# Seven-product blocks whose pairs are added in PSUM: a decoder layer in split float32 on one core

## Chip, cores and metric

One core of one Trainium2 chip runs the whole kernel. The metric is the device time of one execution in microseconds (us), lower is better; the median of three runs of the kernel before is 1603.2 us (1603.16 to 1603.54).

## What is computed

One decoder layer on 1024 prompt tokens and 8 single-token samples (width 1024, hidden width 2816), all in float32:

```python
z = xn @ w_in                       # 1024 x 7168; xn = rms_norm(x)
u, v, b_gate, c_gate, x_in, r_a, r_b = split(z)
y_a = (gelu(u) * spatial_mix(layer_norm(gelu(v)))) @ w_a_out
y_b = (b_gate * short_conv(c_gate * x_in)) @ w_b_out
h = sigmoid(r_a) * y_a + sigmoid(r_b) * y_b
x = x + rms_norm(h @ w_o)
f = (silu(xf @ w_gate) * (xf @ w_up)) @ w_down      # xf = rms_norm(x)
x = x + rms_norm(f)
```

The outputs are the layer's result for prompt and samples, the last rows of the convolution input, and the normed v of the samples.

## The kernel before

**Arithmetic.** Each float32 operand is split in two parts of reduced width, hi and lo. A product takes three passes on TensorE (hi x hi, hi x lo, lo x hi). ScalarE writes hi of the weights and of late operands (`hi`, line 1240, and `t_split`, line 1583), GpSimd writes lo of the weights (`rest`, line 1095), VectorE writes lo of the operands (`t_rest`, line 2385, and others of that form).

**Blocks.** A large product is cut in blocks of 256 weight columns. Each block is a two by two product of half matrices. A seven-product block does it with seven products instead of eight (Strassen's scheme in Winograd's form); it needs sums of the weight quarters (`sums`, lines 1822 to 1841, VectorE) and sums of the operand's quarters, called totals. A plain block does eight (`half`, four results of two products each). The plain blocks are the first two u blocks, B_A, B_B, B_F and B_UP0, and the first block of each of the three down sets, B_D, B_D+4 and B_D+8. A run is one pass over a block; the last down block is done in two runs of half size. A product on 2 x 258 columns with kp = 4 takes 4 x 3 x 2 = 24 matmuls, one with kp = 3 takes 18, one of a half-size run 12.

**Results of a seven-product run.** The seven products 0 to 6 go to the four PSUM regions in the order PBANK = Z, W, Y, X, Z, Y, X. ScalarE copies product 0 to SBUF (`s1`, line 1251). VectorE then adds, each time with one operand from PSUM: `c11` (line 1847), `u1` (1853), `u3` (1858), `u2` (1864), `c22` (1869), `c12` (1875), `c21` (1880). TensorE waits in `product`: product 4 for `s1`, product 5 for `c11`, product 6 for `u1`; the first use of a region by a new block waits for what read it last (`bank_free`).

**Order.** Every engine has its program written out by hand, with semaphores. What matters here:

- ScalarE, run after run: `s1(r)`, then hi of the seven weight places of the next block (`prepare`), the last of which waits for product 6 of run r; between these come what the stage wants of it (gelu, sigmoid, silu, splits, in the last down set `sq_gain`). In the last r_b run (B_A-1) `a_split(1)` stands ahead of `s1`; in block B_B `bt_split(3)` and a weight part stand ahead of `s1(B_B+1)`; at the third block of a down set `t_split` of the next set's first operand stands ahead of `s1`; in the last down set the last `sq_gain` of a block, which waits for its `c21`, stands ahead of the next `s1`, and before the last run a table load too.
- VectorE: in the last r_b run `a_rest(0)`, `at_total(0)`, `c11`, `a_rest(1)`, `u1`, `u3`, `at_total(1)`, `u2`, `a_rest(2)`, `c22`, `c12`, `c21`. In the up runs it multiplies with silu (`hidden`, line 2420) and forms the totals of the hidden rows (`hidden_total`, line 2394) after `c21`.
- The down product is summed over three sets of hidden rows, kp = 3, 4, 4 (K_FIRST). The operands of a set, four rows and four totals, come back from DRAM into eight slots of SBUF, 516 KB in each of two transfers, while the set before ends (`operand_load`, line 976, on SyncE's queue), are split by ScalarE (`t_split`) and VectorE (`t_rest`). In sets 1 and 2 the block's results are added to the sums in g (`gather`, line 2484).
- In the last half-size run TensorE sums the squares of the first half's result after product 3 (`y_total`, line 735); `y_root_of` on VectorE (2526 to 2530) follows, ahead of `u2` of that run.

## Time and profile before

| | |
|---|---|
| median of three runs | 1603.2 us |
| profiled execution | span 1601.0 us, and 2.2 us around it to the median |
| PE busy | 1590.6 us, 99% |
| DVE busy | 1081.9 us, 68% |
| ACT busy | 559.8 us, 35% |
| POOL busy | 703.9 us, 44% |
| chain that ended last | PE 95%, of it line 414 (the three-pass matmuls) 91% |
| granted TensorE clock | 0.999 of full speed over the span |

PE is TensorE, DVE VectorE, ACT ScalarE, POOL GpSimd; SP's queue issues the transfers. Line 414 is the matmul of `three`. The chain is followed back from the last instruction, so an engine that stands in it at 95% has next to no wait in front of it.

### The profile page before, as it was taken

The numbers are of one execution on the slowest core, as the hardware profiler recorded it, in microseconds if no ns is written. First come the engines' busy times: TensorE is split into PE (matmuls) and PEld (weight loads), VectorE is DVE, ScalarE is ACT, GpSimd is POOL, SyncE is SP. The second block draws the span as 40 slices with busy tenths as digits, with TensorE's granted clock in tenths as the row PEclk, the third lists the DMA queues.
The fourth block names the chain that finished last, engine by engine and source line by source line (L and its number), as shares of the span: only waits on it lengthen the run. The fifth ranks groups of instructions, "written<-read, shape, count | busy, mean of one in ns | idle before, by whom it ended". The sixth has DMA issues, their size and how long they took to land.

```text
span 1601.0 us, 30253 instructions
## 1 busy us (share of the span) xinstructions
PE 1590.6 (99%) x12427; PEld 1542.2 (96%) x12427; DVE 1081.9 (68%) x1463; ACT 559.8 (35%) x852; POOL 703.9 (44%) x512
## 2 busy tenths in 40 slices
PE   9999999999999999999999999999999999999998
PEld 6889999999999999999978999999999999999997
DVE  8757857797793338868965666766666666575766
ACT  4222332222223336333434532333332233352544
POOL 1011534544544444644730324544444443545375
PEclk9999999999999999999999999999999999999999
DMA  6202011431423333474423313533333345472723
GB/s 216 79 1 80 27 54 34 126 96 44 126 82 110 109 106 121 149 242 133 148 91 120 131 41 110 155 105 100 106 104 104 105 124 178 153 239 80 238 107 133
DMA packets 155283, 184.38 MB, mean 115 GB/s; under 512 B 7355, under 2 KB 138035, under 8 KB 155147
## 3 DMA queue, kind: packets, MB, share of 16 engines
q1 hardware_dynamic: 154987, 182.41, 35.7%
q8 instruction: 99, 1.62, 0.4%
q14 instruction: 37, 0.30, 0.1%
q10 hardware_dynamic: 160, 0.04, 0.0%
HBM read 133.74 MB, written 48.72 MB: 114 GB/s over the span
## 4 chain that ended last, share of the span: by engine, by line
PE 95%; DVE 1%; DMA 1%; POOL 1%; issue 1%; SPq 0%; ACT 0%; DVEq 0%; ACTq 0%; POOLq 0%
PE ps L414 91%; PE ps L449 1%; PE ps L526 1%; DMA pre_gain<-in_mix_pre_g 1%; DVE tp L2213 1%; PE ps L669 0%; PE ps L653 0%; PE ps L424 0%; DMA tp_f<-hid_dram 0%; SPq L783 0%; DVE s_bc L2232 0%; POOL ring_lo L1108 0%; POOL ring_lo L1095 0%; PE ps L503 0%; DVE g L2234 0%
## 5 line engine op out<-in xcount | busy, mean ns | idle before, releaser
L414 PE MATMUL ps<-tp,ring_hi 128*128 128x258 f32 x7292 | 1182.9, 283 | 0.5 <-issue 0.3
L414 PEld LDWEIGHTS ps<-tp,ring_hi 128*128 128x128 f32 x7292 | 1010.6, 190 | 0.9 <-issue 0.5
L414 PE MATMUL ps<-tp,ring_lo 128*128 128x258 f32 x3646 | 744.8, 283 | 0.0
L414 PEld LDWEIGHTS ps<-tp,ring_lo 128*128 128x128 f32 x3646 | 571.3, 190 | 0.0
L1095 POOL TENSOR_TENSOR ring_lo<-ring_f,ring_hi 128x512 fp32r<-128x512 f32 (+1 forms) x228 | 328.3, 1460 | 365.1 <-DVE ring_f L1840 212.5
L1095 POOL TENSOR_TENSOR ring_lo<-stage,ring_hi 128x512 fp32r<-128x512 f32 (+1 forms) x199 | 304.7, 1540 | 400.3 <-ACT ring_hi L1240 399.6
L1240 ACT ACTIVATE ring_hi<-ring_f 128x512 fp32r<-128x512 f32 (+1 forms) x228 | 142.6, 627 | 519.9 <-DVE ring_f L1835 196.2
L1240 ACT ACTIVATE ring_hi<-stage 128x512 fp32r<-128x512 f32 (+1 forms) x199 | 122.0, 617 | 121.1 <-PE ps L414 63.5
L1832 DVE TENSOR_TENSOR ring_f<-stage 128x512 f32<-128x512 f32 (+1 forms) x57 | 46.8, 821 | 135.2 <-PE ps L414 82.7
L1853 DVE TENSOR_TENSOR s_a<-ps,s_a 128x516 f32<-128x516 f32 (+1 forms) x58 | 39.8, 686 | 51.9 <-PE ps L414 51.4
L414 PE MATMUL ps<-tp 128*128 128x512 f32 (+1 forms) x384 | 72.0, 340 | 0.0
L414 PEld LDWEIGHTS ps<-tp 128*128 128x128 f32 x384 | 59.0, 189 | 8.2
L2385 DVE TENSOR_TENSOR tp<-tp_f,tp 128x2064 fp32r<-128x2064 f32 (+1 forms) x24 | 56.2, 2343 | 13.7 <-ACT tp L1583 13.7
L1251 ACT ACTIVATE s_a<-ps 128x516 f32<-128x516 f32 (+1 forms) x58 | 34.2, 590 | 77.3 <-PE ps L414 60.2
L1864 DVE TENSOR_TENSOR s_a<-ps,s_a 128x516 f32<-128x516 f32 (+1 forms) x58 | 39.6, 683 | 30.5 <-PE ps L414 30.4
L1583 ACT ACTIVATE tp<-tp_f 128x2064 fp32r<-128x2064 f32 (+1 forms) x24 | 42.8, 1784 | 39.8 <-DMA tp_f<-hid_dram 33.2
L414 PE MATMUL ps<-wv_hi_t,tp 128*128 128x512 f32 x192 | 54.1, 397 | 0.0
L2420 DVE TENSOR_TENSOR hq<-hq,q 128x516 f32<-128x516 f32 x40 | 47.0, 1176 | 1.1
L1835 DVE TENSOR_TENSOR ring_f<-ring_f,stage 128x512 f32<-128x512 f32 (+1 forms) x57 | 42.8, 751 | 2.2 <-PE ps L414 2.2
L414 PEld LDWEIGHTS ps<-wv_hi_t,tp 128*128 128x128 f32 x192 | 35.7, 188 | 8.0
L1837 DVE TENSOR_TENSOR ring_f<-stage 128x512 f32<-128x512 f32 (+1 forms) x57 | 39.6, 695 | 0.0
L1847 DVE TENSOR_TENSOR s_bc<-ps,s_a 128x516 f32<-128x516 f32 (+1 forms) x21 | 14.0, 668 | 36.8 <-PE ps L414 36.6
(243 smaller groups left out, 1453.9 us busy)
## 6 DMA issues: line engine op xcount, KB each, us to landing
stage<-in_w_in SPq DMA_DIRECT2D x24, 1024.0 KB, 5.9
ht_dram<-ht SPq DMA_DIRECT2D x44, 258.0 KB, 4.2
hid_dram<-hq SPq DMA_DIRECT2D x40, 258.0 KB, 3.1
stage<-in_w_gate SPq DMA_DIRECT2D x10, 1024.0 KB, 6.6
stage<-in_w_up SPq DMA_DIRECT2D x10, 1024.0 KB, 5.3
tp_f<-hid_dram SPq DMA_DIRECT2D x16, 516.0 KB, 5.5
tp_f<-ht_dram SPq DMA_DIRECT2D x16, 516.0 KB, 8.7
stage<-in_w_down SPq DMA_DIRECT2D x8, 1024.0 KB, 7.1
```

The lines of the kernel that those rows point to most:

```text
L414: ins = pe.matmul(o, w, xc, start=first and n == 0, stop=last and n == 2)
L1095: pool.tensor_tensor(lo, src, hi.bitcast(f32), SUB).then_inc(w_lo, 1)
L1240: act.activation(w_ring(b, p, kp)[0], src, ACT.Copy).then_inc(w_hi, 1)
L1251: act.activation(s_a[:, gs], reg(Z, gs), ACT.Copy).then_inc(s1_done, 1)
L1583: act.activation(slot(s, 0, both, ks), slot_f(s, 1, both, ks), ACT.Copy).then_inc(t_hi, 1)
L1832: ins = dve.tensor_tensor(out, a21, a22, ADD)
L1835: ins = dve.tensor_tensor(out, ring(ring_f, b, 1, kp), a11, SUB)
L1837: ins = dve.tensor_tensor(out, a11, a21, SUB)
L1853: dve.tensor_tensor(s_a[:, gs], reg(X, gs), s_a[:, gs], ADD).then_inc(u1_done, 1)
L1864: dve.tensor_tensor(s_a[:, gs], reg(Z, gs), s_a[:, gs], ADD).then_inc(u2_done, 1)
L2385: dve.tensor_tensor(slot(s, 1, both, ks), slot_f(s, 1, both, ks), slot_v(s, 0, both, ks), SUB).then_inc(t_lo, 1)
L2420: dve.tensor_tensor(hq[:, n], hq[:, n], q[:, n], MUL).then_inc(hid_ready, 1)
```

## The change

- **Regions.** PBANK becomes Y, W, Y, Z, X, Z, X. Product 2 is added by TensorE onto product 0 in Y, after `s1` has copied product 0; product 6 is added onto product 4 in X, after `c22` has read it. So `c11` is no addition any more: the region is read where its value is used (ScalarE's gelu, sigmoid, silu or copy, or VectorE's multiplication or the addition into g). `u1`, `u3`, `u2` and `c22` become `u2`, `u4` and `c22`: five additions of a run for seven. The copies of `s1` alternate between two buffers (`s_turn`).
- **Waits.** Product 2 waits for `s1`, product 5 for `u2`, product 6 for `c22`.
- **Order of products.** Where a seven-product run follows on another (`piped`), product 0 of the next run stands ahead of product 6 of this one.
- **Down blocks.** B_D, B_D+4 and B_D+8 become seven-product blocks. The operand slots form a wheel: position p of a set goes into the slot that position p-1 of the set before left. The loads, `t_split` and `t_rest` follow the positions. In sets 1 and 2 three additions of SBUF onto SBUF (the parts onto g) stand between `u4` and `c22`, and the last addition of each result goes straight into g.
- **Two additions change place:** `at_total(1)` in the last r_b run behind `c22`, and the last tap of the convolution in a b run behind `c22`.

The diff, cut to its core:

```diff
-PBANK = [Z, W, Y, X, Z, Y, X]
+PBANK = [Y, W, Y, Z, X, Z, X]
+D_WHEEL = [5] + SLOTS_B
+SLOTS_D = [[D_WHEEL[(p - n) % 8] for p in range(7)] for n in range(3)]
-QORDER.update({b: FIRST_HALF_EVEN for b in (B_D, B_D + MP, B_D + 2 * MP)})
+def piped(run):
+    return 2 < run < len(RUNS) - 1 and RUNS[run][0] not in QORDER and RUNS[run + 1][0] not in QORDER
...
             def product(r, p):
+                if p == 6 and piped(r):
+                    issue(r + 1, 0)
+                if p or not piped(r - 1):
+                    issue(r, p)
+
+            def issue(r, p):
                 b, gs = RUNS[r]
                 pe.wait_ge(w_lo, lo_at(b, p))
-                if p == 4:
+                if b in (B_D, B_D + MP, B_D + 2 * MP):
+                    pe.wait_ge(t_lo, 7 * ((b - B_D) // MP) + p + 1)
+                if p == 2:
                     pe.wait_ge(s1_done, SIDX[r])
                 elif p == 5:
-                    pe.wait_ge(c11_done, SIDX[r])
+                    pe.wait_ge(u2_done, SIDX[r])
                 elif p == 6:
-                    pe.wait_ge(u1_done, SIDX[r])
+                    pe.wait_ge(c22_done, SIDX[r])
...
-                                kp == 0, kp == kps(b) - 1)
+                                kp == 0 and p not in (2, 6), kp == kps(b) - 1, p in (2, 6))
...
-                act.activation(s_a[:, gs], reg(Z, gs), ACT.Copy).then_inc(s1_done, 1)
+                act.activation(s_turn[r % 2][:, gs], reg(Y, gs), ACT.Copy).then_inc(s1_done, 1)
...
                 if last:
                     a_rest(1)
-                u1(r)
-                u3(r, q[:, 1])
+                u2(r)
+                u4(r, q[:, 1])
                 sums(r + 1, 1)
                 if last:
+                    a_rest(2)
+                c22(r, q[:, 3], q[:, 1])
+                sums(r + 1, 2)
+                if last:
                     at_total(1)
-                u2(r)
-                if last:
-                    a_rest(2)
-                c22(r, q[:, 3])
-                sums(r + 1, 2)
                 c12(r, q[:, 1])
...
+                dve.tensor_tensor(c_22, c_22, s_c[:, gs], ADD).then_inc(d_part, 1)
+                dve.tensor_tensor(c_12, c_12, s_c[:, gs], ADD).then_inc(d_part, 1)
+                dve.tensor_tensor(c_21, c_21, s_turn[r % 2][:, gs], ADD).then_inc(d_part, 1)
+                dve.wait_ge(prod_done, done(r, 4))
+                dve.wait_ge(d_part, parts + 1)
+                dve.tensor_tensor(c_22, reg(X, gs), c_22, ADD).then_inc(c22_done, 1)
```

New in ScalarE's program: `c11_act` (gelu, sigmoid, silu or copy of region Y). The places of `a_split`, `bt_split(3)`, the last `sq_gain` and the table load ahead of `s1` are as before; `t_split` of the first operand of a set still stands ahead of `s1` of the last block before it. In block B_D `t_rest` of position 5 stands ahead of `u2`, and that of position 6 behind `u4`.

## Rows read from the trace of the kernel before

**Rows 1.** The page's head and PE's share.
```profile
span 1601.0 us, 30253 instructions
...
PE 1590.6 (99%) x12427; PEld 1542.2 (96%) x12427; DVE 1081.9 (68%) x1463; ACT 559.8 (35%) x852; POOL 703.9 (44%) x512
```
**Rows 2.** The chain in order of time: start us, us, what.
```profile
199.54 303.78 PE ps L414 x2520
...
1421.17 157.82 PE ps L414 x1308
```
**Rows 3.** PE's waits: us in total, times, longest us.
```profile
PE ps L414 <- POOL ring_lo L1108: 0.3, 1, 0.3
```
**Rows 4.** ACT in order of time, 608 to 612: start us, us, line, operation.
```profile
608.36 0.64 ACT L1342 ACTIVATE q<-q 128x516 f32<-128x516 f32 x1
608.90 1.99 ACT L1337 ACTIVATE tp<-gv 128x1024 fp32r<-128x1024 f32 x2
...
610.90 0.58 ACT L1251 ACTIVATE s_a<-ps 128x516 f32<-128x516 f32 x1
```
**Rows 5.** DVE in order of time, 607 to 625.
```profile
607.63 0.70 DVE L1880 TENSOR_TENSOR q<-ps,s_a 128x516 f32<-128x516 f32 x1 [1.53 <-PE ps L414]
611.03 2.50 DVE L2088 TENSOR_TENSOR tp<-gv,tp 128x1024 fp32r<-128x1024 f32 x2 [2.70 <-ACT tp L1338]
...
620.81 3.45 DVE L2100 TENSOR_TENSOR tp_f<-gv,tp_f 128x1024 f32<-128x1024 f32 x2
```
**Rows 6.** ACT in order of time, 739 to 742.
```profile
739.23 1.92 ACT L1394 ACTIVATE tp<-tp_f 128x2064 fp32r<-128x2064 f32 x1
...
741.57 0.58 ACT L1251 ACTIVATE s_a<-ps 128x516 f32<-128x516 f32 x1
```
**Rows 7.** DVE in order of time, `u1` of the last b run.
```profile
787.02 0.70 DVE L1853 TENSOR_TENSOR s_a<-ps,s_a 128x516 f32<-128x516 f32 x1 [0.74 <-PE ps L414]
```
**Rows 8.** DVE in order of time, the rest of an operand in the last a run.
```profile
706.20 2.31 DVE L2153 TENSOR_TENSOR tp<-tp_f,tp 128x2064 fp32r<-128x2064 f32 x1 [1.66 <-ACT tp L1390]
```
**Rows 9.** DVE in order of time: `c21` and last totals of two up runs.
```profile
987.40 0.70 DVE L1880 TENSOR_TENSOR hq<-ps,s_a 128x516 f32<-128x516 f32 x1 [0.92 <-PE ps L414]
...
992.76 2.59 DVE L2394 TENSOR_TENSOR ht<-hq,ht 128x516 f32<-128x516 f32 x2
...
1352.28 0.69 DVE L1880 TENSOR_TENSOR hq<-ps,s_a 128x516 f32<-128x516 f32 x1
...
1355.74 1.51 DVE L2394 TENSOR_TENSOR ht<-hq,ht 128x516 f32<-128x516 f32 x2
```
**Rows 10.** The instructions on tile tp_f, 1330 to 1530: duration ns min/median/max.
```profile
L2385 DVE TENSOR_TENSOR tp<-tp_f,tp x24: 1759/2304/3404, 1342.6 to 1523.9; 128x2064 fp32r<-128x2064 f32 x16, 128x1548 fp32r<-128x1548 f32 x8
```
**Rows 11.** ACT in order of time, 1400 to 1402.
```profile
1400.00 1.92 ACT L1583 ACTIVATE tp<-tp_f 128x2064 fp32r<-128x2064 f32 x1
1401.82 0.57 ACT L1251 ACTIVATE s_a<-ps 128x516 f32<-128x516 f32 x1
```
**Rows 12.** DVE in order of time, `c21` of the last full-size and first half-size run.
```profile
1563.27 0.70 DVE L1880 TENSOR_TENSOR s_bc<-ps,s_a 128x516 f32<-128x516 f32 x1 [0.99 <-PE ps L414]
...
1573.30 0.43 DVE L1880 TENSOR_TENSOR s_bc<-ps,s_a 128x258 f32<-128x258 f32 x1 [0.51 <-PE ps L414]
```
**Rows 13.** ACT in order of time, ahead of the last two `s1`.
```profile
1565.82 0.71 ACT L1634 ACTIVATE g<-g,par 128x516 f32<-128x516 f32 x1
1566.43 0.37 ACT L1251 ACTIVATE s_a<-ps 128x258 f32<-128x258 f32 x1
...
1575.43 1.28 ACT L1692 ACT_TABLE_LOAD   x1
...
1576.83 0.37 ACT L1251 ACTIVATE s_a<-ps 128x258 f32<-128x258 f32 x1
```
**Rows 14.** The first sum of squares on PE, and DVE after its root.
```profile
1578.84 0.95 PE L735 MATMUL ps<-ones,q 128*128 128x1 f32 x8
...
1581.46 0.43 DVE L1864 TENSOR_TENSOR s_a<-ps,s_a 128x258 f32<-128x258 f32 x1
```

More of the change, by code:

```diff
@@ L87, in places @@
         return [3, 4, 5, 6]
-    return [0, 1, 2, 3] if b in QORDER else list(range(7)) if B_UP0 < b < B_D else TURNED
+    return [0, 1, 2, 3] if b in QORDER else list(range(7)) if b > B_UP0 else TURNED
 def freed(b, pos):
@@ L409, in _, with three @@
         def _(pe):
-            def three(outs, w_h, w_l, x_h, x_l, first, last):
+            def three(outs, w_h, w_l, x_h, x_l, first, last, onto=False):
                 ins = None
@@ L413, in three @@
                     for o, xc in zip(outs, x):
-                        ins = pe.matmul(o, w, xc, start=first and n == 0, stop=last and n == 2)
+                        ins = pe.matmul(o, w, xc, start=first and n == 0, stop=last and n == 2, skip_group_check=onto)
                 return ins
@@ L2483, in gather, with down_rest @@
-            def gather(m, b, src, gs, ready):
-                dve.tensor_tensor(g[:, m, b, gs], g[:, m, b, gs], src[:, gs], ADD).then_inc(ready, 1)
-            def down_rest(r, ready, count, n=None):
-                b, gs = RUNS[r]
-                m = 2 * ((b - B_D) % MP)
-                nb = b + 1 if r < R_LAST else B_D
+            def down_rest(r, n=None, first=None):
+                b, gs = RUNS[r]
+                run = r - FIRST_RUN[B_D + MP]
+                m, parts = 2 * ((b - B_D) % MP), 3 * run
+                nb = b + 1 if r < R_LAST else None
+                c_11, c_12, c_21, c_22 = (g[:, m + a, c, gs] for a, c in ((0, 0), (0, 1), (1, 0), (1, 1)))
+                if first is not None:
+                    t_rest(first, 4)
@@ L2490, in down_rest @@
                 sums(nb, 0)
                 if n is not None:
[L2492 to L2499 removed]
+                    t_rest(n, 0)
+                dve.wait_ge(prod_done, done(r, 2))
+                dve.tensor_tensor(c_11, reg(Y, gs), c_11, ADD).then_inc(d_c11, 1)
@@ L2500, in down_rest @@
+                if first is not None:
+                    t_rest(first, 5)
+                u2(r)
+                u4(r, s_c[:, gs])
                 sums(nb, 1)
+                if first is not None:
+                    t_rest(first, 6)
                 if n is not None:
-                    t_rest(n, 4)
+                    t_rest(n, 1)
                 if r > R_LAST:
                     y_root_of(0)
-                u2(r)
-                dve.wait_ge(ready, count + 1)
-                c22(r, s_b[:, gs])
+                dve.wait_ge(u4_done, SIDX[r])
@@ L2511, in down_rest @@
-                dve.wait_ge(c22_done, SIDX[r])
-                gather(m + 1, 1, s_b, gs, ready)
-                c12(r, s_c[:, gs])
+                    t_rest(n, 2)
+                dve.wait_ge(prod_done, done(r, 5))
+                dve.wait_ge(d_part, parts + 2)
+                dve.tensor_tensor(c_12, reg(Z, gs), c_12, ADD).then_inc(c12_done, 1)
                 sums(nb, 3)
-                dve.wait_ge(c12_done, SIDX[r])
-                gather(m, 1, s_c, gs, ready)
-                dve.wait_ge(ready, count + 2)
@@ L2518, in down_rest @@
-                c21(r, s_b[:, gs])
-                dve.wait_ge(c21_done, SIDX[r])
-                gather(m + 1, 0, s_b, gs, ready)
+                if n is not None:
+                    t_rest(n, 3)
+                dve.wait_ge(prod_done, done(r, 6))
+                dve.wait_ge(d_part, parts + 3)
+                dve.tensor_tensor(c_21, reg(X, gs), c_21, ADD).then_inc(c21_done, 1)
             def y_root_of(n):
@@ L2558, in _ @@
                 sums(b + 1, 2)
-                if last:
-                    t_rest(1, 6)
+                if mp == MP - 1:
+                    t_rest(1, 2)
                 c12(r, g[:, m, 1])
                 sums(b + 1, 3)
+                if mp == MP - 1:
+                    t_rest(1, 3)
+                if mp == 0:
+                    dve.wait_ge(hid_saved[2], 16 * J)
                 c21(r, g[:, m + 1, 0])
-            t_end(1, FIRST_RUN[B_D + MP])
-            for i in range(3):
-                down_rest(FIRST_RUN[B_D + MP + 1 + i], d_tmp, 4 * i, 2 if i == 2 else None)
```

501 lines of the change are left out of this document (260 added, 241 removed).

## Prediction

> **What bounds the kernel now.** I read the page first: TensorE is busy for 1590.6 of 1601.0 us [rows 1]. A busy row alone says little, so the chain in order of time comes next. It is one unbroken stretch of line 414 after the other: 2520 matmuls in 303.78 us, and 1308 in 157.82 us near the end [rows 2]. That is 0.1205 us a matmul in either, without a gap. TensorE's own waits confirm it: three of 0.3 us at line 414, one of which stands here, are all that the matmuls waited between start and tail [rows 3]. So each matmul taken away is worth 0.1205 us, and nothing done to DVE, ACT or POOL can gain more than these 0.9 us. What the change can lose is any wait that becomes too short. With 0.1205 us, a product of 24 matmuls takes 2.89 us, one of 18 (set 0 of down) 2.17, one of 12 (the two last runs) 1.45.
>
> **What it removes.** The three plain down blocks have eight products and get seven: (3 + 4 + 4) x 6 = 66 matmuls, 66 x 0.1205 = **7.95 us**. Of the three small waits two stand at the change of sets, where the order is new, one in the o stage behind DVE, which sheds two additions a run: I take all three as gone, 0.85 us, together **8.8 us**. The two additions fewer on DVE (0.7 us each [rows 5]) lie beside the matmuls and give nothing by themselves. A product that is added onto another has the same matmuls, so it is costed at nothing.
>
> **What it adds: shorter waits.** Before, product 4 needed `s1`; its copy had four products of time. Now product 2 needs it, and the next run's product 0 stands ahead of this run's product 6. So counted from the end of product 6 (call it E), `s1` has exactly one product: 2.89, 2.17 or 1.45 us. ACT's queue ahead of `s1` decides. In an ordinary run that is the last weight part (it waits for E) and `s1`, some 1.2 us: enough. Products 5 and 6 have one product's time for `u2` and (where the next product 0 comes between) two for `c22`; in an ordinary run DVE is idle there. So the bulk of the kernel should run as before. The places with more in the queue:
>
> - *Last r_b run.* ACT has sigmoid, `a_split(1)`, `s1`, and sigmoid waits for `c21`. Before, `c21` began at 607.63 and `s1` ended at 610.90 + 0.58 = 611.48 [rows 4, 5], 3.9 us after E. All of it hangs on E, which moves with the order; 3.9 - 2.89 = **1.0 us** lost. Then `a_rest(0)`, `at_total(0)`, ACT's `at_split(0)`, sigmoid, `a_split(2)`, DVE's `a_rest(2)` and `c22` follow each other, 9 us on from there plus 2.5 to 3.5 us for `a_rest(2)` (the two lengths that operations of this size have) [rows 5], while product 6 would start 12.5 us after E: 0.5 to 1.5 us, taken **1.4**, as POOL prepares weights just then. Last, `at_total(1)` now stands ahead of `c12`, and the following plain block begins in region Z, which `c12` frees: 2.4 (or 4.6) + 0.7 against one product of 2.89, so 0.2 to 2.4, taken **0.3**.
> - *Last a run.* The rest of an operand ends at 706.20 + 2.31 = 708.5 [rows 8], `c22` behind it at 709.2. From `u1` at 787.0 [rows 7], four products into its run, I count back two runs, the plain block and a product: product 6 wants to start at 708.9. **0.4** (0 to 0.5).
> - *First b run.* It follows a plain block, so its `s1` has product 1 alone. By the same counting back product 1 ends at 740.7; `s1` ended at 741.57 + 0.58 = 742.15, after `bt_split(3)` [rows 6]. **1.5** (1.4 to 1.6).
> - *Up into down.* DVE now has in the last up run five `t_rest` for three, then `sums`, `t_rest(5)`, `u2` in B_D. Counting back from 1421.17 [rows 2] B_D began at 1351.9; position 5 is now due at 1362.9. I lay DVE's operations after each other from product 2 (1340.5) on with 0.6 to 0.7 us for one of 516 columns and 1.76 us for a `t_rest` of 1548 [rows 10]: `u2` ends at 1363.0. The same end of an up run (`c21` to last total) took 4.9 us before the plain block, with POOL nearly idle, and 7.9 us where POOL had seven weight places to prepare [rows 9]. B_D has seven now, with three quarters of the columns, and with a drawn-out first part too `u2` ends at 1366.3. 0.1 to 3.4, taken **1.6**.
> - *`t_split` ahead of `s1`* at the last block of set 0: at 1400.00 it took 1.92, `s1` ended at 1402.39 [rows 11]; E was at 1399.5, so 2.9 us against 2.17: **0.8**. At the last block of set 1 against 2.89: **0.15**.
> - *Sets 0 to 1 and 1 to 2.* ACT's `t_split(4)`, behind weight sums that wait for DVE, ends in `s1` some 0.3 to 1.5 us late the first time, 0 to 0.5 the second; DVE's load is seven `t_rest` of 2.3 to 3.4 us [rows 10], three additions and all else, in two blocks: `c22` of the first block may be up to 1.4 late. Taken **1.1** and **0.2**.
> - *Into the half-size runs.* `c21` began at 1563.27 [rows 12]. Without the gather it is followed at 0.75 by square and gain, then `s1` of 0.37: ready 2.4 us after E (spacing as in rows 13), against 1.45: **0.95**. Into the last run the queue is `c21` (0.43 [rows 12]), square, gain, table load 1.28 [rows 13], `s1`: 3.15 us after E against 1.45: **1.7**.
> - *Root before `c22`.* DVE came out of the root at 1581.46, 2.6 us after the sum began at 1578.84 [rows 14]. Now three additions and `c22`, 4 x 0.44, stand behind it, so product 6 can go at 4.4 us, but TensorE is there at 0.94 + 2 x 1.45 = 3.85: **0.6**.
>
> The sum is 2.7 + 0.4 + 1.5 + 1.6 + 0.95 + 1.3 + 2.65 + 0.6 = **11.7 us**; the low ends give 7.3, the high ends some 19.5.
>
> **Transfers.** A set with kp = 4 brings seven operands of 2 x 516 KB where it brought eight, but they are wanted within one block. The slot of position p comes free seven to eight products before it is wanted, 18 us; the trace landed one in 5.5 us, and six with the weights fill some 22 us of a window of 29, so the queue on SP doesn't end last. If it did, each late operand would show as ACT waiting in `t_split`.
>
> A port shared by DVE and POOL fits the two lengths: a two-input SBUF operation took 1.5 us for two when POOL was idle, 2.6 beside it [rows 9]. The Trainium skill states it as an exclusive lock (SBUF — State Buffer, the section on the shared port pair), under which an operation that reads PSUM isn't held up. This speaks against this change: it takes away additions that read PSUM and moves `t_rest` and gathers, which read SBUF twice, under POOL's seven weight parts. By the rule alone the up-to-down place costs towards 3.4 and the set changes towards their high ends, by the undisturbed rows near nothing; the trace agrees with it in the rows named.
>
> **Sum.** Against the profiled span: 1601.0 - 8.8 + 11.7 = 1603.9. The median stands 2.2 above the span: **1606.2 us**, 3.0 above 1603.2. What this kernel's measurement can tell from no change I take as 0.2%, 3.2 us: 1600.0 to 1606.4. The forecast is in that band, at its upper edge.
>
> **Rivals.**
> 1. *Low ends everywhere* (ACT and DVE meet no POOL at the critical places): 1603.2 - 8.8 + 7.3 = 1601.7. For it: several of my late operations are late by under 0.5 us.
> 2. *The waits hold* and the matmuls taken away are the result: 1603.2 - 8.8 = 1594.4; with only the tail's stalls (3.3 us) 1597.7. For it: TensorE's queue is in front by whole products nearly everywhere. Against it: the ACT rows of three places put `s1` behind its date on rows alone.
> 3. *DVE falls behind at the operand changes* (the other side: slower). One mechanism: seven `t_rest`, drawn from 2.3 to 3.4 us beside POOL, ahead of `u2` and `c22`. In two blocks of 40.5 us DVE has some 37 us of work; with all `t_rest` long it is 45, and from the point where it exceeds 40.5 TensorE waits for it block by block: 3 to 4 us at each of the two set changes and 3.4 at B_D, in place of 2.9 in all, so 1606.2 + 7 = 1613.
> 4. *It doesn't do what it says*: were the down blocks' seventh products late by their operands, the 66 matmuls would be paid back as ACT's waits for DMA, 1611. The 18 us of lead speak against it.
>
> **How the numbers follow.** Forecast (1603.5 to 1609) 0.42; rival 1 (1600 to 1603.5) 0.18; rival 2 (under 1600) 0.20; rivals 3 and 4 (over 1609) 0.15 and 0.05. Of the forecast's chance a little over half lies below 1606.4. So faster 0.20, same 0.40, slower 0.40. The range takes in rival 3 and the upper part of rival 2: 1598 to 1613.
>
> **What the profile after would show.** TensorE: 66 matmuls fewer, and in its waits rows at line 414's successor for ACT's copy (`s1`) in the last r_b run, the first b run and both half-size runs, about 1.0, 1.5, 0.95 and 1.7 us; for DVE's `c22` in the last r_b run and the last run, and for `t_rest` or `u2` in B_D. The bulk, from 230 to 600 us and in the up blocks, shows no wait. The prediction is wrong if TensorE waits in ordinary runs (then each of some 50 runs pays), or if `s1` comes in time at the places named (then 1597 or less).

## The result and the profile after

The changed kernel takes **1625.2 us** (median of four runs, 1624.2 to 1626.9) against 1603.4 us (1603.2 to 1603.6) for the kernel before on the same chip: a ratio of 1.0136, 95% interval 1.0121 to 1.0150. It is slower by 22 us, where I had forecast 1606.2 and a range of 1598 to 1613. The time lies outside the range, 12 us above its upper end. The runs further down were made on several chips, on which the kernel before took 1603.4 to 1604.1 us; each ratio is to the kernel before on its own chip.

The head of the page after, then pieces of its chain (start us, us, what):

```profile
span 1622.5 us, 30039 instructions
PE 1590.2 (98%) x12361; PEld 1539.0 (95%) x12361; DVE 999.9 (62%) x1371; ACT 556.4 (34%) x865; POOL 714.1 (44%) x521
```
```profile
199.32 304.00 PE ps L430 x2520
503.43 107.08 PE ps L430 x888
...
628.59 71.19 PE ps L430 x576
703.36 8.33 DMA tp_f<-ob_dram
716.74 32.08 PE ps L430 x264
...
922.03 428.23 PE ps L430 x3552
```

Against [rows 1], TensorE has the 66 matmuls fewer (12361 for 12427), and VectorE 82 us less work. Its busy time fell by 0.4 us only, where 66 matmuls are 8: part of the matmuls must have run slower. The first long piece is that of [rows 2]: the same 2520 matmuls, 304.00 us for 303.78. The up blocks are one piece too, 3552 matmuls at 0.1206 us. So the pairs added in PSUM and the new order of products cost nothing that can be seen in an ordinary run. What is new comes after 600 us: the chain is cut in pieces, and between them stand a transfer, VectorE and ScalarE. The kernel before had three waits of 0.3 us there (one of them in [rows 3]); now TensorE's waits are (us in total, times, longest us):

```profile
PE ps L430 <- ACT s_bc L1308: 5.5, 6, 1.5
PE ps L430 <- DVE g L2550: 4.7, 3, 2.2
PE ps L430 <- ACT s_a L1308: 4.2, 3, 1.8
PE ps L430 <- DVE s_a L1932: 3.3, 1, 3.3
PE ps L430 <- DVE s_a L1943: 2.5, 1, 2.5
PE ps L430 <- DVE q L1943: 2.3, 1, 2.3
```

L1308 is `s1`, L1932 `u2`, L1943 and L2550 the two forms of `c22`. These are 15 waits, 22.5 us, where the prediction had 11.7. The four that I had most wrong or that matter below, one by one (in brackets the wait and what ended it):

```profile
628.59 0.73 PE L430 MATMUL ps<-tp,ring_hi 128*128 128x258 f32 x4 [2.29 <-DVE q L1943]
716.74 0.72 PE L430 MATMUL ps<-tp,ring_hi 128*128 128x258 f32 x4 [2.51 <-DVE s_a L1943]
1376.00 0.73 PE L430 MATMUL ps<-tp,ring_hi 128*128 128x258 f32 x4 [3.27 <-DVE s_a L1932]
1539.20 0.72 PE L430 MATMUL ps<-tp,ring_hi 128*128 128x258 f32 x4 [2.18 <-DVE g L2550]
```

Stretches of 8 us around them (us, PE busy (instructions), granted clock, DMA share, GB/s):

```profile
616.00:624.00 8.00, 8.00 (x69) 1.00 0.35 108
624.00:632.00 8.00, 5.71 (x40) 0.86 0.33 106
632.00:640.00 8.00, 8.00 (x64) 0.92 0.38 134
712.00:720.00 8.00, 5.49 (x46) 1.00 1.10 352
1376.00:1384.00 8.00, 8.00 (x54) 0.79 0.27 86
1448.00:1456.00 8.00, 5.78 (x37) 0.79 0.04 12
```

This is the second part of the loss. After three of the waits the granted clock falls to the lower of its two levels (1.2 GHz for 2.4) for a while: the window from 1376 us is busy all through and does 54 matmuls instead of 69. (1 - 0.79) x 8 is 1.7 us, and (0.14 + 0.08) x 8 as well. In the kernel before no window between 200 and 1590 us was under 1.00.

The books: 1601.0 (span before) - 7.95 - 0.85 + 22.5 of waits + 5.1 for three falls gives 1619.8; 1622.5 was measured. Of the 2.7 us still missing the restarts after the other twelve waits make 2.6. A restart is what a wait costs besides itself where the clock stays up, 0.22 us by the held copies below; in the price of a fall, 1.7 us, it is contained.

### The profile page after: what moved, and what is told of

Same layout as the page of the kernel before. It is cut to its first block, busy times and chain, and to the rows that moved or that the text cites. A ratio compares the mean times of both kernels' runs of the same rounds, so it can differ in the third digit from the quotient of the medians.

```text
span 1622.5 us, 30039 instructions
## 1 busy us (share of the span) xinstructions
PE 1590.2 (98%) x12361; PEld 1539.0 (95%) x12361; DVE 999.9 (62%) x1371; ACT 556.4 (34%) x865; POOL 714.1 (44%) x521
## 4 chain that ended last, share of the span: by engine, by line
PE 89%; DVE 5%; issue 2%; ACT 2%; DMA 1%; POOL 0%; SPq 0%; DVEq 0%; ACTq 0%; POOLq 0%
PE ps L430 84%; DVE tp L2446 2%; PE ps L465 2%; PE ps L542 1%; DMA tp_f<-ob_dram 1%; PE ps L714 0%; PE ps L698 0%; ACT tp L1658 0%; PE ps L440 0%; DVE g L2545 0%; DMA gv<-in_w_in 0%; DVE ring_f L1920 0%; ACT tp L1410 0%; ACT q L1717 0%; ACT ring_hi L1278 0%
## 5 line engine op out<-in xcount | busy, mean ns | idle before, releaser
L1133 POOL TENSOR_TENSOR ring_lo<-ring_f,ring_hi 128x512 fp32r<-128x512 f32 (+1 forms) x240 | 348.4, 1473 | 354.7 <-DVE ring_f L1925 211.3
L1133 POOL TENSOR_TENSOR ring_lo<-stage,ring_hi 128x512 fp32r<-128x512 f32 (+1 forms) x196 | 293.8, 1509 | 416.1 <-ACT ring_hi L1278 415.7
L1278 ACT ACTIVATE ring_hi<-ring_f 128x512 fp32r<-128x512 f32 (+1 forms) x240 | 150.0, 625 | 536.3 <-DVE ring_f L1920 179.3
L1917 DVE TENSOR_TENSOR ring_f<-stage 128x512 f32<-128x512 f32 (+1 forms) x60 | 58.1, 969 | 102.2 <-DMA stage<-in_w_in 52.0
L1954 DVE TENSOR_TENSOR q<-ps,s_a 128x516 f32<-128x516 f32 x17 | 11.8, 696 | 72.2 <-PE ps L430 72.2
L1922 DVE TENSOR_TENSOR ring_f<-stage 128x512 f32<-128x512 f32 (+1 forms) x60 | 52.3, 871 | 0.0
L1932 DVE TENSOR_TENSOR s_bc<-ps,s_bc 128x516 f32<-128x516 f32 (+1 forms) x31 | 21.3, 686 | 47.0 <-PE ps L430 46.9
L1932 DVE TENSOR_TENSOR s_a<-ps,s_a 128x516 f32<-128x516 f32 (+1 forms) x30 | 20.5, 685 | 42.7 <-PE ps L430 42.7
L1925 DVE TENSOR_TENSOR ring_f<-stage,ring_f 128x512 f32<-128x512 f32 (+1 forms) x60 | 40.3, 671 | 0.0
L1658 ACT ACTIVATE tp<-tp_f 128x2064 fp32r<-128x2064 f32 (+1 forms) x21 | 37.4, 1780 | 6.1 <-DMA tp_f<-hid_dram 4.7
L1949 DVE TENSOR_TENSOR q<-ps,q 128x516 f32<-128x516 f32 x24 | 16.7, 694 | 26.6 <-PE ps L430 26.6
```

Source lines behind the costliest of these rows:

```text
L1133: pool.tensor_tensor(lo, src, hi.bitcast(f32), SUB).then_inc(w_lo, 1)
L1278: act.activation(w_ring(b, p, kp)[0], src, ACT.Copy).then_inc(w_hi, 1)
L1658: act.activation(slot(s, 0, both, ks), slot_f(s, 1, both, ks), ACT.Copy).then_inc(t_hi, 1)
L1917: ins = dve.tensor_tensor(out, a21, a22, ADD)
L1922: ins = dve.tensor_tensor(out, a11, a21, SUB)
L1925: ins = dve.tensor_tensor(out, a12, ring(ring_f, b, 3, kp), SUB)
```

## The theories

**Theory A**: the loss is local. At 15 places a step that now has one product of time stands in a queue behind work that used to have four, and after some waits the clock falls too. **Rival B**: the PSUM pairs or the order of products cost something throughout. **Rival C** (rival 3 of the prediction): VectorE has too much to do at the changes of operands. **Rival D** (close to rival 4): transfers are late. Since all the waits are queue order by theory A, it can be tested by moving work alone: e1 to e5, e8 and e9 issue the same operations as the changed kernel, in another order.

## Three queues, one at a time, and together

ScalarE's order (e1), at the seven places of `s1`; two of them:

```diff
-                if last:
-                    a_split(1)
                 s1(r)
                 if last:
+                    a_split(1)
                     a_split(0)
...
             s1(R_LAST)
-            for e in range(12, 16):
+            for e in range(11, 15):
                 sq_gain(e)
-            act.activation(warm, eps, ACT.Sqrt)
             s1(R_LAST + 1)
+            sq_gain(15)
+            act.activation(warm, eps, ACT.Sqrt)
```

> ScalarE's order alone is changed: at seven places the copy of the first product (s1) is issued ahead of a split, a square or a table load that stood before it; nothing is added or taken out. Theory A (the loss lies in waits at single places, each made by what is queued ahead of one step): the waits of 1.14, 1.47, 0.95, 0.28, 0.22, 1.44 and 1.81 us go, 7.3 us; those of 1.41 and 0.99 us at the two changes of operands go too, but VectorE's queue there is without a gap, so its waits of 2.22 and 2.18 us grow by as much. Time 1617.5 us (1615 to 1620). Rival B (the pairs in PSUM or the new order of products cost time all along the loops): the waits seen are not the loss, 1623 to 1625. No fall of the granted clock was behind these waits, so the windows with 0.79 to 0.92 stay.

Measured: 1622.0 us (1620.5 to 1622.6), ratio to before 1.0112 (1.0097 to 1.0128), so 3 us better than the changed kernel, not 7 to 8. All nine waits of `s1` were gone or under 0.3 us. But TensorE then met the next late step:

```profile
628.87 0.72 PE L430 MATMUL ps<-tp,ring_hi 128*128 128x258 f32 x4 [3.62 <-DVE q L1946]
1452.18 1.20 PE L430 MATMUL ps<-tp,ring_hi 128*128 128x258 f32 x4 [3.14 <-DVE g L2553]
1538.31 1.20 PE L430 MATMUL ps<-tp,ring_hi 128*128 128x258 f32 x4 [3.21 <-DVE g L2553]
```

These were 2.29, 2.22 and 2.18 us: VectorE's chain has its own date, and what TensorE doesn't wait for `s1` it waits for `c22`. The wait for the late load (716.7 us) grew from 2.51 to 2.94 us as well. The sum of waits fell by 5.0 us only, and the longer waits now all had a fall of the clock behind them, five places instead of three. That the changes of sets would hand a wait on I had foreseen, for 628 us not, and the two new falls not at all.

VectorE's order (e2), its main edits:

```diff
-                if last:
-                    a_rest(2)
                 c22(r, q[:, 3], q[:, 1])
+                if last:
+                    a_rest(2)
...
                 dve.tensor_tensor(c_22, c_22, s_c[:, gs], ADD).then_inc(d_part, 1)
-                dve.tensor_tensor(c_12, c_12, s_c[:, gs], ADD).then_inc(d_part, 1)
-                dve.tensor_tensor(c_21, c_21, s_turn[r % 2][:, gs], ADD).then_inc(d_part, 1)
                 dve.wait_ge(prod_done, done(r, 4))
                 dve.wait_ge(d_part, parts + 1)
                 dve.tensor_tensor(c_22, reg(X, gs), c_22, ADD).then_inc(c22_done, 1)
+                if first is not None:
+                    sums(nb, 1)
+                dve.tensor_tensor(c_12, c_12, s_c[:, gs], ADD).then_inc(d_part, 1)
+                dve.tensor_tensor(c_21, c_21, s_turn[r % 2][:, gs], ADD).then_inc(d_part, 1)
```

> VectorE's order alone: in the last r_b run the addition of C_22 ahead of the third operand's rest; three totals of the hidden rows behind the first down block's second addition; in the down blocks the additions for C_12 and C_21 (and, at the two changes of operands, one weight sum) behind that of C_22. Theory A: the waits of 2.29, 3.27, 2.22 and 2.18 us go (9.7 us with 0.3 us of the last run's), and where three of them stood (all but the 2.18) the granted clock no longer falls, some 5 us more: 1610 us (1608 to 1614). If the falls of the clock are not made by the waits: 1615. Rival C (VectorE is short of time at the changes, whatever its order): the waits move to the next product and 1620 to 1625 is left.

Measured: 1622.2 us (1620.8 to 1622.5), ratio 1.0114 (1.0101 to 1.0128): 3 us, where theory A promised 15. The waits named did go (`c22` at 1452 and 1539 us wholly, `u2` from 3.27 to 0.76), and three came: 2.30 us for `c12` at 631.8 us, behind the `a_rest(2)` that I had moved in front of it; 1.56 us for `c22` in the first down block; and

```profile
1544.56 0.71 PE L430 MATMUL ps<-tp,ring_hi 128*128 128x258 f32 x4 [2.84 <-ACT s_bc L1308]
```

since `sums(nb, 1)`, moved back, held up ScalarE's splits and the squares behind them. The wait for the late load grew too, from 2.51 to 3.20 us, with a fall of the clock behind it. The step after the one repaired is what I had again not priced.

SyncE's order (e3). The edit was made wrongly: `ob_load(3)` went ahead of the other load, but behind its wait for VectorE. Its main part:

```diff
                         sp.wait_ge(a_gated, 4 * (b - 2 - B_A - (b > B_B)) + i + 1)
                     if b == B_B:
                         bt_load(i)
+                    elif b == B_B - 1 and i == 3:
+                        sp.wait_ge(prod_done, done(b, 0))
+                        ob_load(3)
```

> SyncE's order alone: in the last a run but one, the load of the w_b operand's rows into the slot that the first product frees is issued ahead of the load that waits for VectorE's gate of C_21. Theory A: the one wait of 2.51 us at 716.7 us goes, and the clock did not fall there: 1622.5 us (1621.5 to 1623.5). Rival D (the load's transfer itself is late, not its issue): no change, 1625.

Measured: 1625.0 us (1621.7 to 1627.4), ratio 1.0132 (1.0118 to 1.0146), no change. Even so the load was issued at 701.57 us, 1.8 us earlier than in the changed kernel, and the wait of 2.51 us was gone, which speaks against rival D. It came back in other places: 0.91 us for GpSimd at 720.0 us, and 2.90 us for `s1` in the first b run, where it had been 1.47, with a fall of the clock behind it. The waits together are 22.2 us for 22.5. It was done again as e8. The spread of this kernel's runs, 5.7 us, also shows that the 3 us of e1 and of e2 are little more than can be told.

All three sets of moves together (e4):

> The three together. Theory A: of the 22.5 us of waits, 2 to 3 us are left, the clock falls nowhere in the loops and some 2 us of restarts go: 1597 us (1595 to 1601), under the kernel before (1603.4) by the 8 us of the 66 matmuls that are gone less what is left. Rival B: 1615 and over.

Measured: **1612.6 us** (1610.7 to 1613.7), ratio 1.0055 (1.0042 to 1.0068). One by one they gave 3, 3 and 0 us, together 12.6: this is the mark of waits in series, where either queue alone only hands over to the other. The trace has 12.5 us of waits and one fall left, and the books close to 1 us: the waits fell by 10.0 us, the falls by 3.4, the span by 12.6. Rival B would have left 1615 and over. But my 1597 was wrong, as it took every repaired wait for gained.

## The load behind another's wait

At the start of the last a run, whose rest of an operand [rows 8] shows, SyncE's queue after (start us, us):

```profile
693.11 9.68 SPq L924 DMA_DIRECT2D q<-ra_dram  x3
702.83 0.43 SPq L851 DMA_DIRECT2D stage<-in_w_b_out  x1
703.36 5.44 SPq L907 DMA_DIRECT2D tp_f<-ob_dram  x3
```

The third load of `q` waits for VectorE's gate of the `c21` of the run before (it ended at 702.43), and `c21` now comes one product later, since the seventh product does. The `ob_dram` load behind it, 696.50 in the kernel before, goes at 703.36, and ScalarE waits for it:

```profile
711.71 1.94 ACT L1465 ACTIVATE tp<-tp_f 128x2064 fp32r<-128x2064 f32 x1 [10.73 <-DMA tp_f<-ob_dram]
```

The edit (e8), rightly this time (its second part takes `ob_load(3)` out of its old place):

```diff
                     else:
+                        if b == B_B - 1 and i == 3:
+                            sp.wait_ge(prod_done, done(b, 0))
+                            ob_load(3)
                         sp.wait_ge(a_gated, 4 * (b - 2 - B_A - (b > B_B)) + i + 1)
```

> What the third run was meant to be: SyncE issues the load of the w_b rows ahead of its own wait for VectorE's gate of C_21 (there it stood behind that wait, and so was issued as late as ever). Theory A: the issue moves some 5 us earlier, the wait of 2.51 us at 716.7 us goes, but the gates' loads and VectorE's plain parts of the next block set its end, so that the waits at 720 us and 750 us take half of it back: 1624 us (1622.5 to 1625.5). Rival D (the transfer, not its issue, is late): 1625 and the wait stays.

Measured: **1620.4 us** (1619.0 to 1620.7), ratio 1.0100 (1.0086 to 1.0114). The load went at 695.60 us, ScalarE had it at 701.38, and the wait was gone, with nothing in its place but 0.40 us for GpSimd at 818.5. So the issue was late, not the transfer: rival D is out here. What I had expected back at 720 and 750 us didn't come, and the time lies under my range. The 4.8 us are more than the wait of 2.5: this kernel's profiled run also had no fall of the clock after the waits of 2.29 us at 628.8 and 2.17 us at 1448.8, where the changed kernel had one each:

```profile
624.00:632.00 8.00, 5.71 (x48) 5.54 (x47) 7.68 (x9) 1.40 (x2) 4.00 (x2) 1.00 0.35 115
```

(PEld, DVE, ACT and POOL stand between PE and the clock here.) The same wait, to 0.01 us, was followed by 1.00 here and by 0.86 above. Up to that place the two programs are the same. So a wait of this length has a price that changes by 1.7 us from one execution to another.

## The seventh product in its own place

One part of the change undone (e6): the next run's product 0 no longer comes ahead of the seventh.

```diff
 def piped(run):
-    return 2 < run < len(RUNS) - 1 and RUNS[run][0] not in QORDER and RUNS[run + 1][0] not in QORDER
+    return False and 2 < run < len(RUNS) - 1 and RUNS[run][0] not in QORDER and RUNS[run + 1][0] not in QORDER
```

> The changed kernel with one part undone: every block's seventh product comes right behind its sixth again, not behind the next block's first. The pairs in PSUM, the wheel and the additions stay. Product 2 then comes one product (2.9 us in most blocks) after s1's source is there, in place of two, and the seventh one product after C_22's source. Theory A: at the 14 places where something is queued ahead of s1 or C_22 the wait grows by up to 2.9 us each, the other some 60 blocks have 1.2 to 2 us of work to do in 2.9 us and stay whole: 1650 us (1635 to 1680). Rival B (the new order is itself what costs): faster than the changed kernel, 1600 to 1620.

Measured: 1625.0 us (1623.0 to 1626.5), ratio 1.0130 (1.0116 to 1.0144): the same as the changed kernel, and theory A's 1650 was badly off. The waits are others:

```profile
1445.34 1.20 PE L430 MATMUL ps<-tp,ring_hi 128*128 128x258 f32 x4 [3.78 <-DVE g L2550]
...
1534.63 1.20 PE L430 MATMUL ps<-tp,ring_hi 128*128 128x258 f32 x4 [4.05 <-DVE g L2550]
...
1597.84 0.48 PE L430 MATMUL ps<-tp,ring_hi 128*128 128x258 f32 x2 [0.36 <-ACT s_a L1308]
```

`c22` has one product less and costs 1.6 to 1.9 us more at the changes, and it now makes TensorE wait 1.05 to 2.16 us in the last block of the first and of the second set and in two blocks of the third. One of these, 1.81 us at 1420.3 us, has a fall of the clock behind it (0.62 from 1420 to 1424 us). But `s1` into the last run waits 0.36 us for 1.81, the load of w_b's rows 0.38 for 2.51. I had overlooked that the next run's product 2 starts at the same time in either order, while product 6 ends one product earlier. So what ScalarE has queued on it ahead of `s1` is done sooner, and so is `c21`, and with it gate, square and transfer. By these rows the new place of the seventh product buys time for `c22` and pays for it at `c21`.

If so, it should be worth something once what hung on `c21` has been moved out of the way. That kernel is next.

## A second round of moves

From e4's trace (waits of 3.01, 1.96, 1.57, 1.49 and 1.10 us) followed: in the last r_b run `c12` too ahead of `a_rest(2)`, and `at_total(1)` behind `c21`; `s1` of the first b run waits for three parts of h, not four, and goes ahead of the last splits; e8's load; in B_D both last `t_rest`, `u2`, one total, `u4`, and only then what nothing waits for; in the third set the next `s1` ahead of two squares. Two of the edits, against the changed kernel (VectorE's order in the last r_b run, where `a_rest(1)` moves back too, and ScalarE's in the first b run):

```diff
-                if last:
-                    a_rest(1)
                 u2(r)
                 u4(r, q[:, 1])
+                if last:
+                    a_rest(1)
                 sums(r + 1, 1)
...
                 c12(r, q[:, 1])
+                if last:
+                    a_rest(2)
                 sums(r + 1, 3)
                 c21(r, q[:, 2])
+                if last:
+                    at_total(1)
...
-            prepare(B_B + 1, 4, 6)
-            bt_split(3)
-            prepare(B_B + 1, 6)
+            prepare(B_B + 1, 4, 5)
             s1(B_B + 1)
+            prepare(B_B + 1, 5)
+            bt_split(3)
```

> A second round of order changes, made from the waits that the first combined kernel still showed (12.3 us in all, and one fall of the clock worth 1.7 us): in the last r_b run C_12 and C_21 are added ahead of the operand's rest and total that stood before them; s1 of the first b run goes ahead of the last weight splits and waits for three of the four parts of h; the load of the w_b rows is now really ahead of the wait for C_21's gate; VectorE's work at the first down block is spread so that u2 and C_22 come before what nothing waits for; s1 of the third set's second block goes ahead of two squares. Nothing is added to the computation or left out. Theory A: 3 to 5 us of waits are left, the clock falls nowhere: 1602 us (1599 to 1606), at or under the kernel before. If what is left in the first combined kernel is a cost of the loops themselves (rival B): no better than 1610.

Measured: **1602.2 us** (1601.8 to 1602.6), ratio 0.9988 (0.9979 to 0.9997), as expected. Waits of 5.4 us are left between 600 and 1590 us, and in that stretch the clock does not fall. One more move (e9):

```diff
-            prepare(B_A + 1, 3)
-            for r in range(B_A + 1, B_B):
-                s1(r)
+            prepare(B_A + 1, 3, 5)
+            s1(B_A + 1)
+            prepare(B_A + 1, 5)
+            for r in range(B_A + 1, B_B):
+                if r > B_A + 1:
+                    s1(r)
```

> The second combined kernel with one more move: at the first a run, s1 goes ahead of the last two weight splits, behind which it made TensorE wait 1.16 us. Theory A: that wait goes and nothing comes in its place: 1601.0 us (1600.3 to 1602). If the splits are then late: 1602.2, no change.

Measured: **1600.6 us** (1600.3 to 1601.3), ratio 0.9980 (0.9971 to 0.9988), the fastest of all and 0.2% under the kernel before. Its seven waits at line 430 for ScalarE and VectorE are 3.5 us in all, none over 0.9. So the 22 us were lost by the places of steps in the queues: the changed kernel's operations in another order are 3.2 us faster than the kernel before.

Then the two tests of what e5 rests on. The seventh product in its own place again, now in e5's kernel (the same edit of `piped`):

> The second combined kernel with every block's seventh product right behind its sixth. In the changed kernel this made no difference (1625.0 against 1625.2): C_22 then has one product less before it is waited for, while C_21, and what stands behind it in the queues, comes one product earlier. Here the steps that C_21 held up have been moved out of its way, so only the loss should be left: C_22 at the two changes of operands and at the first down block, late by 0.5, 0.5 and 0.9 us now, would be late by 2.2 to 2.9 us more each, 8 us, with some falls of the clock, 3 to 5 us: 1614 us (1609 to 1618). Rival: the two orders are worth the same whatever stands in the queues: 1602.

Measured: **1609.5 us** (1609.1 to 1610.9), ratio 1.0035 (1.0022 to 1.0048), 7.2 us over e5. The waits are mostly `c22`'s: 2.71 us in the first down block, 1.82 in the last block of the first set, 2.26 and 2.27 at the changes, 1.14 in the last block of the second set, with one fall of the clock. So the new place of the seventh product is worth 7 us once nothing urgent hangs on `c21`, and nothing that can be told before that. My 1614 had counted two to three falls.

And the price of the matmuls (e11), in `issue`, for p = 3 of the first block of each set:

```diff
+                if b in (B_D, B_D + MP, B_D + 2 * MP) and p == 3:
+                    for kp in range(4):
+                        three(outs, w_h[:, kp % kps(b)], w_l[:, kp % kps(b)],
+                              *([tp[:, s, part, n, kp % kps(b), 0:CS] for n in range(gs.start, gs.stop)] for part in range(2)),
+                              True, True)
                 for kp in range(kps(b)):
```

> The second combined kernel with 72 useless matmuls of 128x258, 24 ahead of the fourth product of the first block of each of the three sets, where the kernel before has 66 more than the changed one (their output is overwritten by the product's own first). It prices the one gain that the prediction counted: 72 by 0.1205 us is 8.7 us, if TensorE sets the time there: 1610.9 us (1610 to 1612). If the vector engines set it at these blocks, as the waits of 0.5 to 0.9 us left there hint, the extra work covers those waits, up to 3.6 us of them: 1607.5 us.

Measured: **1606.7 us** (1606.5 to 1607.0), 4.4 us over e5, not 8.7. Of e5's waits in the down blocks (0.88, 0.59, 0.47, 0.47, 0.40, 0.21, 0.49 us) only one is left, and the chain is whole again from there to the tail, 0.1205 us a matmul:

```profile
1378.34 204.68 PE ps L430 x1698
```

8.7 us less 2.9 us of waits and the restarts of six of them (1.2) is 4.6. So rival C holds in a small form: at these three blocks VectorE, with ScalarE waiting on its sums, sets the time, and the matmuls that the change takes away were the cover of its work. Of the 7.95 us that I counted in full, about half can be had there with VectorE's present load: 66 x (4.4 / 72) = 4.0 us, an estimate from this run.

## What a wait costs besides itself

The changed kernel with useless copies ahead of `s1` in 16 blocks of the up loop, where there is no wait otherwise (e7):

```diff
+            def hold(r, n):
+                act.wait_ge(prod_done, done(r, 0))
+                act.wait_ge(c21_done, SIDX[r - 2])
+                for _ in range(5 + n):
+                    act.activation(s_turn[r % 2][:, :], reg(Y, both), ACT.Copy).then_inc(held, 1)
+                    holds.append(r)
+                    act.wait_ge(held, len(holds))
```

> A measurement of waits and of the clock, in the changed kernel: in 16 blocks of the up loop, which has no waits now, 5 to 10 useless copies stand ahead of s1 on ScalarE, one more from block to block and then from 5 again. TensorE should wait some 0.8, 1.4, 2.0, 2.7, 3.3 and 3.9 us in turn (three times the first four, twice the last two), 32 us. Theory A1 (the granted clock falls after a wait of more than about 2.2 to 2.9 us, whatever made it): it falls after the four waits over 2.9 us, not after those of 2.0 us and less, and after some of those of 2.7 us; each fall costs 1.7 to 3.4 us: 1667 us (1662 to 1672). Theory A2 (the falls belong to the places where they were seen, VectorE beside GpSimd or the operands' transfers, not to the wait): none in the up loop, 1657 us.

Measured: 1706.9 us (one run), span 1705.2, 82.7 over the changed kernel's. The waits were longer than meant, 1.64 to 5.48 us and 54.3 in all. The first seven:

```profile
1005.27 0.71 PE L430 MATMUL ps<-tp,ring_hi 128*128 128x258 f32 x4 [1.64 <-ACT s_a L1308]
1028.69 0.72 PE L430 MATMUL ps<-tp,ring_hi 128*128 128x258 f32 x4 [2.94 <-ACT s_bc L1308]
1053.56 0.91 PE L430 MATMUL ps<-tp,ring_hi 128*128 128x258 f32 x4 [2.90 <-ACT s_a L1308]
1079.75 1.20 PE L430 MATMUL ps<-tp,ring_hi 128*128 128x258 f32 x4 [4.20 <-ACT s_bc L1308]
1106.59 1.20 PE L430 MATMUL ps<-tp,ring_hi 128*128 128x258 f32 x4 [4.17 <-ACT s_a L1308]
1134.91 1.20 PE L430 MATMUL ps<-tp,ring_hi 128*128 128x258 f32 x4 [5.48 <-ACT s_bc L1308]
1158.92 0.71 PE L430 MATMUL ps<-tp,ring_hi 128*128 128x258 f32 x4 [1.64 <-ACT s_a L1308]
```

They can be read without the clock column. Every row is the same place one block later, 168 matmuls or 20.26 us. What a row's distance to the next has beyond 20.26 and the next wait is what this wait cost besides itself: 1028.69 - 1005.27 - 2.94 - 20.26 = 0.22 us after 1.64 (a restart), 1.71 after 2.94, 1.73 after 2.90, 2.41 after 4.20, 2.58 after 4.17, 2.11 after 5.48. The other places repeat it: 0.2 us after each 1.64, 1.7 after each of 2.9. The windows agree (columns as above): 0.21 x 8 us lost after a wait of 2.94 us, 0.43 x 8 around one of over 4 us, of which a part falls into the wait itself, and 1.00 around those of 1.64.

```profile
1024.00:1032.00 8.00, 5.06 (x35) 0.88 0.68 198
1032.00:1040.00 8.00, 8.00 (x63) 0.91 0.29 100
...
1104.00:1112.00 8.00, 5.41 (x25) 0.57 0.97 284
...
1312.00:1320.00 8.00, 7.48 (x62) 1.00 0.96 294
```

The sum over the 16 is 54.3 + 27.5 = 81.8 us, of 82.7. Theory A1 is right that waits make the falls (A2: none), and my 1667 missed by the longer waits.

Once more with 4 to 6 copies and a shorter last one (e12):

```diff
-                for _ in range(5 + n):
-                    act.activation(s_turn[r % 2][:, :], reg(Y, both), ACT.Copy).then_inc(held, 1)
+                for c in [258] * (n + m // 4) + [8 + 64 * (m % 4)]:
+                    act.activation(s_turn[r % 2][:, :, 0:c], reg(Y, both)[:, :, 0:c], ACT.Copy).then_inc(held, 1)
```

> The measurement of held copies once more, in steps between the 1.64 us after which the granted clock never fell and the 2.90 us after which it always did: in each of 16 blocks of the up loop 4 to 6 useless copies and a shorter one, so that TensorE waits about 1.9, 2.0, 2.1, 2.2, 2.5, 2.6, 2.7 and 2.8 us, once in each of the two kinds of block. If the length of the wait alone decides, the 16 split in one point, shorter ones without a fall and longer ones with. If something else decides too (the elsewhere seen waits of 2.16 to 2.30 us had a fall in some runs and none in others), the two mix, with more falls the longer the wait. Each fall costs 1.7 us: the waits' 38 us, 1 us more at the 716 us place, and 6 to 12 falls, 1674 to 1684 us.

Measured: 1688.3 us (one run), above my 1684, 16 waits from 1.85 to 2.84 us, and falls after 13 of them, where I had 6 to 12: after 1.85, 1.96, 2.00, 2.06, 2.10, 2.17, 2.21 us and after 2.52, 2.59, 2.63, 2.74, 2.81, 2.84; none after 1.89, 2.48 and 2.70. By the distances as above a fall cost 1.6 to 1.8 us each time but once, 2.9 us after the wait of 2.74.

```profile
1203.18 0.72 PE L430 MATMUL ps<-tp,ring_hi 128*128 128x258 f32 x4 [2.48 <-ACT s_a L1308]
1225.84 0.74 PE L430 MATMUL ps<-tp,ring_hi 128*128 128x258 f32 x4 [2.21 <-ACT s_bc L1308]
```

The two are 22.66 us apart, so 0.19 us beyond the wait: no fall after 2.48 us. Length alone doesn't decide between 1.85 and 2.84 us, nor are the longer ones hit more often. What else decides is left open. The other kernels widen the range by a little: a fall after 1.81 us in e6, none after 1.81 and 1.82 us elsewhere, none after 2.71 us (e10) and 2.84 us (e2). The changed kernel's waits of 2.18 to 2.51 us lie in this range: after 2.29 and 2.22 us the clock fell there and not in e8 (2.29, 2.17), after 2.51 us it did not, and in e12 it did after 2.59 at that place.

## Why the prediction was wrong, step by step

The bound, the count of matmuls and the ScalarE places held. What failed are two kinds of terms. The cost of a wait beyond itself, falls of the clock and restarts, stood at nothing and measured 7.7 us. And the steps that hang on VectorE (`c22`, `u2`, and `s1` behind its weight sums) were priced at 3.3 us in the last a run, at B_D and at the two set changes, where the waits were 12.6.

- **"TensorE bounds; 0.1205 us a matmul."** Right: 0.1206 us in the changed kernel, and the bulk whole, as forecast. That killed rival B before any run. (The second row of [rows 2] gives 0.1207, not 0.1205, which changes nothing.)
- **"66 matmuls, 7.95 us."** The count was right; that all of it is time was not (e11). I costed VectorE's load at the set changes only as a late `c22`, not as the thing that sets the end there once its cover is gone.
- **Places read off ACT rows: right.** Last r_b run 1.14 (said 1.0), first b run 1.47 (1.5), `t_split` ahead of `s1` 0.91 (0.8) and 0.28 (0.15), into the last run 1.81 (1.7), root 0.28 (0.6). Into the half-size runs 1.44 (0.95) was low. These came from one queue and one date, counted from product 6.
- **Last r_b run, `c22`:** 2.29 for 1.4; I had 0.5 to 1.5. `a_rest(2)` took 3.46 + 1.23 us beside GpSimd, in place of the 3.5 at most. The wait for region Z (0.3) did not come; it came, as 2.3 and 3.0 us, in e2 and e4, where `a_rest(2)` was moved in front of `c12`.
- **Last a run: 2.51 for 0.4, the first place where a step failed.** I read VectorE's row [rows 8] as a fixed date. It hung on a transfer, whose issue stood in SyncE's queue behind a gate of `c21`. I had noted that product 6 moves back, and had not walked the queues that wait for `c21`. e8 took it away with one moved load.
- **Up into down: 3.27 for 1.6**, near the high end of 3.4. GpSimd ran seven operations from 1355.5 to 1376.1 us, five of them in a row from 1361.9 to 1371.1, and the two `t_rest` beside these were 2.58 us long, not 1.76. `c21` to the last total took 8.3 us (1364.77 to 1373.10), the drawn-out case of [rows 9]. The Trainium skill (SBUF — State Buffer, "Who interferes with whom") says that a VectorE instruction with two SBUF inputs contends with a GpSimd instruction that reads SBUF, and that one with at most one SBUF input, outside its two-port modes, does not. The trace agrees at the first set change: additions of two SBUF operands took 1.78 us beside GpSimd and 0.68 without. Those with a PSUM operand took 0.68 in both cases, at 1451.88 without GpSimd, and at 1442.66 with GpSimd busy from 1440.53 to 1446.87:

```profile
1446.84 3.35 POOL L1133 TENSOR_TENSOR ring_lo<-ring_f,ring_hi 128x512 fp32r<-128x512 f32 x1
...
1448.96 1.78 DVE L2545 TENSOR_TENSOR g<-g,s_bc 128x516 f32<-128x516 f32 x1
1450.67 0.68 DVE L2546 TENSOR_TENSOR g<-g,s_bc 128x516 f32<-128x516 f32 x1
1451.27 0.68 DVE L2547 TENSOR_TENSOR g<-g,s_a 128x516 f32<-128x516 f32 x1
1451.88 0.68 DVE L2550 TENSOR_TENSOR g<-ps,g 128x516 f32<-128x516 f32 x1
```

- **Set changes: 6.8 us for 1.3.** The rows above are of the first of them. All three additions into g stand ahead of `c22` (L2550), where only the first has to, and a `t_rest` of 3.41 us ahead of them. Rival 3 had 3 to 4 us a change and 3.4 at B_D; it came true in size (3.6, 3.2 and 3.3 us) and I had given it 0.15. Its mechanism, more work than VectorE has time for, came true in part only: with the same work in another order (e5) these places keep 1.3, 0.7 and 1.5 us.
- **Falls of the clock: 5.1 us for nothing.** The term was missing. No row of before shows one in the loops, since no wait there is over 0.3 us. None of the waits I forecast reached the 1.81 us from which these runs show falls. The missing term made small errors of the waits into larger ones of the time.
- **Transfers.** A set's seven operands came in time, as said: ScalarE waited at most 2.8 us for one, and none stands in the chain that ended last. But I had taken 5.5 us for each, where the profile of before has a median of 8.7 for the totals. The one late transfer was another.
- **The low ends** add up to 7.7 us, not 7.3, so rival 1 would be 1602.1. That changes nothing.

In sum: waits 22.5 for 11.7 (last a run 2.1 more, set changes 5.5, B_D 1.7, last r_b run 0.7, the rest 0.8), falls 5.1 and restarts 2.6 for nothing. 10.8 + 5.1 + 2.6 is 18.5 us of the 18.6 by which the span (1622.5 for 1603.9) was missed. That these waits are queue order, e5 and e9 show; why a given wait has a fall behind it and another of the same length has none stays open.

## What to carry to other kernels

When a step loses slack, don't date only that step: walk every queue (the loads too) that waits for anything which the edit makes later, and price the step that is late next. Waits in series hide each other: repair both queues before judging either; a part undone in the unrepaired kernel (e6, 0 us) and in the repaired one (e10, 7 us) gave different answers. And time taken from the bounding engine is won only as far as no second engine was living under its cover.

## What the runs showed of the hardware

- A wait of TensorE costs 0.2 us beyond itself where the clock stays up (e7, e12). Where it falls to the lower level the cost is 1.6 to 1.8 us after waits up to 2.9 us, once 2.9 us, and 2.1 to 2.6 us after held waits of 4.2 to 5.5 us. No fall followed a wait of 1.64 us or less in the loops (three held ones and all short ones seen), one followed 13 of the 16 held ones from 1.85 to 2.84 us and some of the others from 1.81 us on, and every one from 2.90 us on.
- Equal waits are not equally treated. After 2.29 us at the same place the granted clock was 0.86 in one kernel's run and 1.00 in another's. That alone moves a time by 1.7 us, with nothing in the code to explain it: up to this place the programs are the same. In e7 and e12, the same up to there too, 2.27 us had no fall and 2.25 us had one.
